# Order of low halves, evictions and copies, the second expert's rows and POOL's gates in a two-layer hybrid decoder trunk

## The reference, cut to what matters

```python
for l in range(2):
    h = rmsnorm(x, norm_mix[l])
    qa, ka, va, qb, kb, vb, qi, ki, wi, qc, kc, vc, g = split(h @ w_in[l])
    o_a = stick_breaking_attention(qa, ka, va)               # 4 heads
    o_b = dsa_attention(qb, kb, vb, qi, ki, wi, bias)        # top 64 keys per query, softmax
    o_c = sliding_window_attention(qc, kc, vc, sinks, bias)  # 8 heads, softmax with sinks
    gates = sigmoid(g + b_gate[l])
    merged = gates[0] * (o_a @ w_pa[l]) + gates[1] * (o_b @ w_pb[l]) + gates[2] * (o_c @ w_pc[l])
    x = x + merged @ w_out[l]
    x = x + cross_attention(rmsnorm(x), rmsnorm(mem), ...)   # 4 heads, 256 memory rows
    hf = rmsnorm(x, norm_ffn[l])
    x = x + (swiglu(hf) if l == 0 else moe_swiglu(hf))       # layer 1: top 2 of 8 experts
```

## Time and profile before

| what | us |
|---|---|
| median of 3 runs (1762.31 to 1764.25) | 1763.64 |
| the profiled execution, its own time | 1761.99 |
| its span, first to last instruction | 1760.4 |
| TensorE busy | 1702.5 (97%) |
| VectorE busy | 1391.7 (79%) |
| ScalarE busy | 1104.0 (63%) |
| POOL busy | 92.9 (5%) |

### The profile page before, as it was taken

The page is one execution under the profiler, slowest core; times in us unless marked ns, Lnnn a source line. Parts: engine busy times, 40 slices in busy tenths (PEclk is TensorE's granted clock), DMA queues, the critical chain, the costliest instruction groups (busy, mean ns, idle before and its releaser), DMA issues.

```text
span 1760.4 us, 22594 instructions
## 1 busy us (share of the span) xinstructions
PE 1702.5 (97%) x7816; PEld 1366.5 (78%) x7816; DVE 1391.7 (79%) x1367; ACT 1104.0 (63%) x1076; POOL 92.9 (5%) x73
## 2 busy tenths in 40 slices
PE   7999898999999999899999999999999999999999
PEld 5777777888777787777888888888888888888876
DVE  5799767545477987668898888888888888888897
ACT  4646355443355453557777777777777777777765
POOL 1100110000001001010000000000000000000440
PEclk9999999999999999999999999999999999999999
DMA  8533494554455335349999999999999999999985
GB/s 301 215 104 130 176 364 149 212 191 169 150 182 182 120 138 204 134 173 399 366 381 366 366 381 369 366 383 365 364 385 363 381 363 368 380 367 366 409 340 195
DMA packets 74113, 498.14 MB, mean 283 GB/s; under 512 B 8256, under 2 KB 9024, under 8 KB 17872
## 3 DMA queue, kind: packets, MB, share of 16 engines
q1 hardware_dynamic: 66560, 467.60, 69.4%
q0 software_dynamic: 7360, 29.87, 4.6%
q10 hardware_dynamic: 144, 0.03, 0.0%
HBM read 481.73 MB, written 15.73 MB: 283 GB/s over the span
## 4 chain that ended last, share of the span: by engine, by line
PE 83%; DVE 8%; ACT 3%; issue 2%; DVEq 2%; DMA 2%; POOL 0%; ACTq 0%; POOLq 0%; SPq 0%
PE ps L588 26%; PE ps L582 26%; PE ps L578 25%; DVE w_lo L416 3%; PE ps L804 1%; ACT w_hi L411 1%; DVE w_lo L1022 1%; PE ps L508 1%; PE ps L1348 1%; DMA rows_of_experts<-scratch,row_no 1%; DVE st L1673 0%; DMA z<-rows_of_experts 0%; DVEq L1676 0%; PE ps L1271 0%; DMA raw<-in_layer_tiles 0%
## 5 line engine op out<-in xcount | busy, mean ns | idle before, releaser
L1022 DVE TENSOR_TENSOR w_lo<-raw,w_hi 128x2048 fp32r<-128x2048 f32 x168 | 391.6, 2332 | 65.9 <-ACT w_hi L939 65.8
L578 PE MATMUL ps<-w_hi,hT_hi 128*128 128x512 f32 (+1 forms) x1520 | 427.1, 403 | 10.4 <-ACT hT_hi L550 4.6
L1022 DVE TENSOR_TENSOR w_lo<-z,w_hi 128x2048 fp32r<-128x2048 f32 x168 | 386.8, 2304 | 45.8 <-ACT w_hi L939 44.7
L588 PE MATMUL ps<-w_lo,hT_hi 128*128 128x512 f32 (+1 forms) x1520 | 413.2, 394 | 7.2 <-DVE w_lo L416 7.1
L582 PE MATMUL ps<-w_hi,hT_lo 128*128 128x512 f32 (+1 forms) x1520 | 413.0, 394 | 1.0 <-DVE hT_lo L557 0.9
L939 ACT ACTIVATE w_hi<-z 128x2048 fp32r<-128x2048 f32 x168 | 321.7, 1915 | 43.2 <-PE ps L588 38.3
L588 PEld LDWEIGHTS ps<-w_lo,hT_hi 128*128 128x128 f32 x1520 | 283.5, 189 | 77.3 <-DVE w_lo L416 9.9
L582 PEld LDWEIGHTS ps<-w_hi,hT_lo 128*128 128x128 f32 x1520 | 284.1, 189 | 70.2 <-DVE hT_lo L557 2.1
L939 ACT ACTIVATE w_hi<-raw 128x2048 fp32r<-128x2048 f32 x168 | 321.0, 1911 | 25.5 <-PE ps L588 25.5
L578 PEld LDWEIGHTS ps<-w_hi,hT_hi 128*128 128x128 f32 x1520 | 272.5, 189 | 67.8 <-ACT hT_hi L550 5.5
L416 DVE TENSOR_TENSOR w_lo<-raw,w_hi 128x2048 fp32r<-128x2048 f32 (+2 forms) x111 | 248.3, 2242 | 77.0 <-ACT w_hi L411 75.2
(11 more groups left out here) (295 smaller groups left out, 993.8 us busy)
## 6 DMA issues: line engine op xcount, KB each, us to landing
z<-in_moe_tiles SPq DMA_DIRECT2D x168, 1024.0 KB, 4.9
raw<-in_moe_tiles SPq DMA_DIRECT2D x168, 1024.0 KB, 4.9
raw<-in_layer_tiles SPq DMA_DIRECT2D x68, 1024.0 KB, 4.9
raw<-in_dense_tiles SPq DMA_DIRECT2D x33, 1024.0 KB, 4.8
rows_of_experts<-z POOLq DMA_DIRECT2D x1, 8704.0 KB, 40.6
raw<-in_layer_tiles SPq DMA_DIRECT2D x8, 512.0 KB, 3.4
z<-rows_of_experts POOLq DMA_DIRECT2D x8, 512.0 KB, 8.1
rows_of_experts<-z POOLq DMA_DIRECT2D x7, 512.0 KB, 6.8
```

The costliest lines, as they stand in the source:

```text
L578: pe.matmul(acc, hi[:, k, cols], wh, start=start and j == 0, stop=False)
L588: ins = pe.matmul(acc, hi[:, k, cols], wl, start=False, stop=stop and j == len(hk) - 1)
L1022: v.tensor_tensor(w_lo[:, ring, :], moe_raw(p), w_hi[:, ring, :].bitcast(F32), ALU.subtract) \
```

## The change

Ten edits. (1) POOL's gate product is a `tensor_tensor` with the gate's column broadcast to 1024 columns, no longer a `tensor_scalar`. (2) `dve_linear` can evict the first tile ahead of the low half; the first input block of layer 1 uses it. (3) For the first expert, TensorE turns the second expert's rows behind the fourth chunk, no longer behind the third, and (4) ScalarE and VectorE take them behind the fourth chunk, no longer inside it. (5) TensorE does an idle product in bank 0 ahead of the second tile's turning and one behind it, and one behind the logits in place of two. (6) At the start of layer 0 ScalarE and (7) VectorE take the first half of the turned input ahead of the first slot's split. (8) In the mixers one low half moves from behind the row maxima of the second tile to in front of them. (9) In the merge, pb's second block evicts its first tile without a low half in front, and the low halves of the pc slots come one eviction later each. (10) In cross-attention VectorE's copy moves ahead of a low half.

```diff
--- before.py
+++ after.py
@@ -345,7 +345,7 @@
                 pool.wait_ge(sem(f"y_back{k}"), 16)
                 if j:
                     pool.wait_ge(sem("x_part"), i + 1)
-                pool.tensor_scalar(yg[:, k, :], yg[:, k, :], g_other[:, j, i:i + 1], None, ALU.mult)
+                pool.tensor_tensor(yg[:, k, :], yg[:, k, :], bc(g_other[:, j, i:i + 1], [P, D]), ALU.mult)
                 pool.drain()
                 pool.tensor_tensor(x_sb[:, i, :], x_sb[:, i, :], yg[:, k, :], ALU.add).then_inc(sem("x_part"), 1)
 
@@ -618,12 +618,13 @@
                 pe_block_slot(pe, s + n, k0 + 4 * h, h == 0, h == per - 1 or plan[s + n][1] == KC, blk0[name, l] + b, x_lo,
                               hi, lo, between[1] if between and between[0] == n else None)
 
-        def dve_linear(v, cnt, name, l, take, limit, b0=0, b1=None):
+        def dve_linear(v, cnt, name, l, take, limit, b0=0, b1=None, take_first=False):
 
             s, nblk, per = slots_of(name, l)
             for b in range(b0, b1 or nblk):
                 last = s + (b + 1) * per - 1
-                ahead(dve_split_to, v, cnt, last - 1, limit)
+                if not take_first:
+                    ahead(dve_split_to, v, cnt, last - 1, limit)
                 blk = blk0[name, l] + b
                 v.wait_ge(sem("tile0_done"), blk + 1)
                 take(b, 0).then_inc(sem("evac"), 1)
@@ -859,8 +860,11 @@
                 pe_moe_chunk(pe, ip, par, 0, 0, ("hg_L", n + 1))
             pe_moe_chunk(pe, ip, par, 0, 1)
             pe_moe_chunk(pe, ip, par, 1, 0)
-            pe_turn_rows(pe, n + 1)
+            if not first_expert(ip, par):
+                pe_turn_rows(pe, n + 1)
             pe_moe_chunk(pe, ip, par, 1, 1)
+            if first_expert(ip, par):
+                pe_turn_rows(pe, n + 1)
             with pe.Fori(2, N_MOE // 2) as u:
                 pe_moe_chunk(pe, ip, par, u, 0)
                 pe_moe_chunk(pe, ip, par, u, 1)
@@ -928,7 +932,9 @@
                 chunk(0, 0)
             chunk(0, 1, None if first else "y")
             chunk(1, 0)
-            chunk(1, 1, "rows")
+            chunk(1, 1, None if first else "rows")
+            if first:
+                hook("rows")
             with fori(2, N_MOE // 2) as u:
                 chunk(u, 0)
                 chunk(u, 1)
@@ -1385,10 +1391,10 @@
                     if i == 1 and b == 0:
                         pe_turn_tile(pe, l, 0)
 
-        def pe_idle_products(pe, n):
+        def pe_idle_products(pe, n, bank=7):
 
             for _ in range(n):
-                pe.matmul(ps[:, 7, :], ident, x_sb[:, 0, 0:NB], start=True, stop=True)
+                pe.matmul(ps[:, bank, :], ident, x_sb[:, 0, 0:NB], start=True, stop=True)
 
         def pe_program(pe):
 
@@ -1445,9 +1451,11 @@
                     pe_turn_half(pe, "mix", x_sb, 0)
                 if l == 0:
                     pe_dense(pe, FFN0[0], N_DENSE, turn_next)
+            pe_idle_products(pe, 1, 0)
             pe_turn_tile(pe, L - 1, 1)
+            pe_idle_products(pe, 1, 0)
             pe_logits(pe, 1)
-            pe_idle_products(pe, 2)
+            pe_idle_products(pe, 1)
             pe.wait_ge(sem("chosen"), 1)
             pe.matmul(ps[:, 6, 0:8], before_tri, chosen[:, 0, :], start=True, stop=True)
             pe.matmul(ps[:, 6, 8:16], ones, chosen[:, 0, :], start=True, stop=False)
@@ -1598,8 +1606,8 @@
                     act.wait_ge(sem("ident_in"), 16)
                     act.activation(warm, ident[:, 0:1], ACT.Copy)
                     act.wait_ge(sem("gains"), 16)
+                    act_hi_gain(act, "mix", l, hT_hi, part=(0,))
                     act_split_to(act, cnt, s0 + 1)
-                    act_hi_gain(act, "mix", l, hT_hi, part=(0,))
                     act.wait_ge(sem("x1_in"), 16)
                     act_squares(act, x_sb, 0, "mix_squares")
                     act_hi_gain(act, "mix", l, hT_hi, part=(1,))
@@ -1766,6 +1774,7 @@
             dve_split_to(v, cnt, g0 + 3)
             dve_gate(v, l, 0, 0)
             dve_masked(v, l, 0, 1, between=0)
+            dve_split_to(v, cnt, g0 + 4)
             dve_row_max(v, l, 1)
             dve_split_to(v, cnt, g0 + 5)
             dve_topk_rounds(v, 0, 1)
@@ -1850,7 +1859,9 @@
                     last = s + (b + 1) * per - 1
                     blk = blk0[name, l] + b
                     for i in range(TT):
-                        if not (j == 1 and b == 0 and i == 1 or j == 2 and b == 1 and i == 1):
+                        if j == 1 and b == 1 and i == 1:
+                            dve_split_to(v, cnt, min(last + RING - 1, lim))
+                        elif not (j == 1 or j == 2 and b == 1 and i == 1) or b == i == 0:
                             dve_split_to(v, cnt, min(last + RING - 1 + i, lim))
                         if i == 0:
                             v.wait_ge(sem("tile0_done"), blk + 1)
@@ -1933,9 +1944,9 @@
             v.drain()
             dve_cross_probs(v, l, 0)
             dve_cross_max(v, l, 1)
-            dve_split_to(v, cnt, s + 3)
             v.wait_ge(sem("x_probs_T"), 2 * l + 1)
             v.tensor_copy(xPT[:, 1, :, 0:P], psXT[0][:, 1, :, :]).then_inc(sem("x_pT_dve"), 1)
+            dve_split_to(v, cnt, s + 3)
             dve_cross_probs(v, l, 1)
             v.wait_ge(sem("x_probs_T"), 2 * l + 2)
             v.tensor_copy(xPT[:, 1, :, P:S], psXT[1][:, 1, :, :]).then_inc(sem("x_pT_dve"), 1)
@@ -2063,10 +2074,9 @@
                 s0 = blocks["in", l]
                 if l == 0:
                     v.wait_ge(sem("gains"), 16)
+                dve_lo_gain(v, "mix", l, hT_hi, hT_lo, part=(0,))
                 if l == 0:
                     dve_split_to(v, cnt, s0 + 1)
-                dve_lo_gain(v, "mix", l, hT_hi, hT_lo, part=(0,))
-                if l == 0:
                     v.wait_ge(sem("mix_squares"), 2)
                     dve_rsqrt(v, "mix", D, norm_rs[:, 0:2])
                     dve_lo_gain(v, "mix", l, hT_hi, hT_lo, part=(1,))
@@ -2081,7 +2091,7 @@
                 v.drain()
                 if l == L - 1:
                     v.wait_ge(sem("rows_put"), 16)
-                dve_linear(v, cnt, "in", l, take_in(v), gate0[l], b1=1)
+                dve_linear(v, cnt, "in", l, take_in(v), gate0[l], b1=1, take_first=l > 0)
                 if l == 0:
                     v.wait_ge(sem("mem0_in"), 16)
                     v.wait_ge(sem("mem_squares"), 2)
```

## The result

The change makes the kernel slower: 1770.69 us median (1769.02 to 1771.03, 7 runs) against 1764.25 (1761.79 to 1767.38, 7 runs) for the kernel before on the same chip. The ratio is 1.0034, 95% interval 1.0024 to 1.0043, which is +6.0 us, between +4.2 and +7.6. The forecast was 1769.5, +5.9.

The account below looks back on a forecast made before the run. TensorE is busy 1702.5 of 1760.4 us, so order can win only its 58 us of standing and clock loss behind stops. Terms -0.8, -1.6, -0.3, +2.9, +5.7 sum to +5.9, so 1769.5 us; range 1762 to 1774.

Parts of the forecast that it names:

- Start: Start of layer 0: copying the turned input before the split lets TensorE start earlier; -0.8 us, bounds -1.3 and 0.
- First eviction of layer 1: First block of layer 1: TensorE's wait moves to the second eviction; 0, bounds -0.3 and +0.3 us.
- Mixers: Low half before the maxima: TensorE's gain is lost at the evictions behind them; 0 per layer, bounds -0.5 and +0.5 us.
- Merge: Merge, both layers: shorter waits for evictions and less half-speed time; together -1.6 us, bounds -4.6 and 0.
- Cross-attention: VectorE's copy runs earlier, but TensorE still needs ScalarE's copy; 0, bounds 0 and +0.6 us per layer.
- Router: Second tile's logits and ranks: VectorE's chain decides and a 0.34 us wait goes; -0.3 us, bounds -1.0 and +0.8.
- Rows: First expert: fetch wait of 1.38 us goes, TensorE stands 3.0 for ScalarE's queued split; +2.9 us, bounds +1.5 and +4.4.
- Gates: Last expert's tail: eight POOL operations hold VectorE 15.7 us, TensorE loses 9.5; +5.7 us, bounds +0.5 and +8.
- that sign: In the tail: the prediction is wrong if TensorE's waits stay near 4 us, where around 9 us was expected.
- rival C: Rows and tail: more half-speed stretches, and POOL between every pair of low halves; +1.5 and +2, 1773 us; chance 0.18.
- Rival A: POOL's gates: the broadcast product holds VectorE no longer than the scalar one; 5.2 us less, 1764.3; chance 0.2.
- Rival B: Mixers, merge, router: TensorE's clock decides and half of 17 us comes back, 1761.0 us; chance 0.12.

Follow-up runs that it names:

- experiment 7: The change without its gates, rows and idle-product edits, against the kernel before: 1762.14 us, ratio 0.9988.
- experiment 8: Experiment 7 with cross-attention left as before, against the kernel before: 1761.70 us, ratio 0.9989.
- experiment 11: Experiment 10 without the edits in the mixers and cross-attention, against the kernel before: 1759.76 us, ratio 0.9980.
- experiment 9: The kernel before with the change's idle products around the second tile's turning and four behind the logits: 1764.32 us, ratio 1.0000.
- experiment 6: The kernel before with only the change's idle-product edits in the router: 1764.91 us, ratio 1.0007.
- experiment 5: The kernel before with the second expert's rows turned behind the fourth chunk but taken inside the fifth, between splits: 1761.10 us, ratio 0.9984.
- experiment 1: The kernel before with only POOL's gate products made products of two tensors, one a broadcast column: 1767.42 us, ratio 1.0017.
- experiment 2: The kernel before with POOL's gate products made products of two whole tensors, gates left out of the output: 1768.98 us, ratio 1.0023.
- experiment 4: The kernel before with only the change's edits to the second expert's rows, turned and copied behind the fourth chunk: 1766.99 us, ratio 1.0019.
- experiment 12: Experiment 10 with the idle products of experiment 9, against the kernel before: 1759.65 us, ratio 0.9977.
- experiment 10: Experiments 5 and 7 together, with scalar gate products and the router as before, against the kernel before: 1760.64 us, ratio 0.9984.

## Why the prediction was right

By its own steps:

- **Start: right in mechanism, too small in size.** -1.06 in the profile, -1.2 and -0.7 in experiments 7 and 8, forecast -0.8; against the seven kernels with the old start it is nearer -1.7, beyond the bound of -1.3. TensorE's first products wait for the split, which follows the copy. They start 5.55 us behind the input in each of the six kernels with the edit, and 6.1 to 6.7 behind it (6.3 before) in the others; the rest is the clock, which comes up to 1.00 between 16.0 and 18.6 us, and between 16.6 and 19.7 in the others:

```profile
9.45 1.57 ACT L550 ACTIVATE hT_hi<-ps,gains 128x256 fp32r<-128x256 f32 x4 [6.14 <-PE ps L508]
10.89 1.93 ACT L411 ACTIVATE w_hi<-raw 128x2048 fp32r<-128x2048 f32 x1
...
12.96 2.05 PE L578 MATMUL ps<-w_hi,hT_hi 128*128 128x512 f32 x4 [3.61 <-ACT w_hi L411]
```

- **First eviction of layer 1: right.** The wait of the earlier trace rows moves to the second eviction and keeps its length, 1.45 for 1.49.

- **Mixers: right, and the trace shows it as forecast.** The 3.39 us behind the maxima are gone, and TensorE waits 3.42 us for the eviction behind them; the product of the probabilities starts at 143.42 where it started at 143.71, with TensorE 0.3 us earlier all along:

```profile
139.57 1.65 PE L578 MATMUL ps<-w_hi,hT_hi 128*128 128x512 f32 x4 [3.42 <-DVE z L1701]
...
143.42 3.36 DVE L1841 TENSOR_TENSOR scratch<-scratch,st 128x3072 f32<-128x3072 f32 x1
```

It said "two or three shorter waits instead of 3.4"; it is one of the same length. The 0 holds for the mixers themselves. But the three kernels that have the edit and the old router lose 0.9 to 1.0 us in the router (experiment 11), which the prediction did not look for.

- **Merge: right.** -0.55 and -0.82, forecast -0.7 and -0.9; none of the six kernels with the edit has a half-speed stretch in either merge, seven of the other eight have one in layer 0's and four in layer 1's. VectorE loses both ties with POOL (3.44 and 3.35 us for a low half), and the waits are 1.16, then 0.85, with 0.46 behind, where 0.95, 1.05 and 0.85 were worked out:

```profile
201.74 3.44 DVE L416 TENSOR_TENSOR w_lo<-raw,w_hi 128x2048 fp32r<-128x2048 f32 x1
...
205.23 1.21 PE L588 MATMUL ps<-w_lo,o_hi 128*128 128x512 f32 x4 [1.16 <-DVE w_lo L416]
...
210.09 1.17 PE L578 MATMUL ps<-w_hi,o_hi 128*128 128x512 f32 x4 [0.85 <-DVE scratch L1873]
```

- **Cross-attention: right**, 0 by experiment 8, as near as it can tell.

- **Router: wrong.** The step reads: "-0.3; bounds -1.0 and +0.8". It was +1.66, and +1.2 alone. That the clock may fall in the stop of 3 us was in it, and that VectorE's chain gains 0.34; but it followed VectorE alone. Behind the ranks TensorE has two idle products and the first expert's turning in its own order, and at half speed it is later than VectorE. Experiment 9 shows the cause by taking the stop away, experiment 6 that a later wait for the fetch can hide half of it (1.6 of 2.8), a cover that the rows' edit removes. Whether a part of the +1.66 comes with the mixers' edit, no run shows.

- **Rows: right**, in mechanism and size. Wait 2.91 (forecast 3.0), +3.1 in the profile and +3.4 alone (forecast +2.9). Experiment 5 shows that it is the split behind the copy.

- **Gates: the mechanism right for VectorE, wrong in part for TensorE, and the size not right.** "Now eight operations hold VectorE like an add: 1.3 for the first [...] and 7 x 2.05, 15.7 in all" is the term that was mis-sized. The excess was 12.2: the first product held VectorE for 0.6 (a low half of 2.89), the other products for 1.35, and the product with a broadcast column lasts 1.90 and not 2.40. TensorE lost 6.5 us against the 9.5 worked out and the 3.8 before, and not all of it by waiting. Its waits were 4.8 us, where the prediction looked for about 9 and called itself wrong if they stayed near 4: by that sign it was nearer to wrong than to right. The other 1.7 us are a half-speed stretch, a term that the sum for the gates left out and only rival C had.

Rival A put the product's price at 0.58; the 1.35 measured lies in the middle between that and the 2.05. The trace contradicts rival A as it stood. It also contradicts the Trainium skill, SBUF — State Buffer, "Who interferes with whom", by which the issue order and not the form of an instruction decides who blocks, so that a scalar product would lock the ports as an add does. Exchanging them cost +3.0 alone (+1.6 to +4.6) where the prediction had about +1 by that rule, and before, experiment 1 and experiment 2 show three prices for three kinds of product: 0.58, 1.35 and 1.84.

Rival B did not come: behind the start the clock is at 1.2 GHz for 34.1 us in all, against 30.7 before. Its list of the stretches left out two of 6.8 us in the cross-attentions. Of rival C, the stretch behind the rows' stop and one behind a stop in the tail are there, but the waits are shorter than it had them.

The sum of the parts measured alone (+3.0 +3.4 +1.2 -2.1 = +5.5) is near the +6.0 of the whole. That the forecast came within 1.2 us of the measured median is in part luck: 3.0 too much for the gates against 2.0 too little for the router, and within the gates a half-speed stretch of 1.7 that made up for part of the waits that did not come.

## What to carry to other kernels

When an engine's item is moved to the end of a stage, look at what its queue holds behind it: the copy of the rows costs 3 us with a split behind it and gains 2.8 one split later. Follow every engine's own queue behind a stop, TensorE's at half speed above all, and not only the chain that ended last before. And price a POOL instruction beside VectorE by the time it takes alone and by what it reads, not by the fact that it is elementwise.

## What the runs showed of the hardware

POOL and VectorE hold each other up in different ways for the two forms. An add or a product of two tensors alternates with the low halves: one goes, the other waits, 3.95 for a product of 1.90 and 4.25 for an add of 2.40. A scalar product lets VectorE pass and is itself drawn out, over two or three low halves; in the profile of experiment 8:

```profile
1669.22 7.01 POOL L348 TENSOR_SCALAR scratch<-scratch,headsT 128x1024 f32<-128x1024 f32 x1
1676.39 2.52 POOL L350 TENSOR_TENSOR x_sb<-x_sb,scratch 128x1024 f32<-128x1024 f32 x1 [0.16 <-issue]
1678.88 7.02 POOL L348 TENSOR_SCALAR scratch<-scratch,headsT 128x1024 f32<-128x1024 f32 x1
```

With 7.0 us the adds come 9.7 us apart, and TensorE waits 2.3 to 2.4 us there (experiments 4, 5, 8 and 12); with 4.9 us for two of the products, as in the profile of before, the first adds come 7.4 to 7.5 apart, and it waits 3.6 to 3.8, or 2.5 with a half-speed stretch of 3.4 us (experiments 6, 10 and 11). Which of the two a run gets differs among kernels that have the same instructions there, and is worth 1.0 to 1.5 us. The gap of 8.1 to 9.6 us behind POOL's first product is there with each kind of product (8.47 in experiment 2, 9.56 after the change); the prediction had it go with the scalar one. It lies inside POOL's drain between the product and the add (L349 before), which takes 12.3 to 12.6 us the first time in all thirteen kernels that have it, and 6.4 to 9.5 later. What the drain waits for stays open.

The half-speed stretches behind TensorE's stops move. The same edit-free place (cross-attention of layer 0) shows a wait of 2.6 or 3.2 us and a step of 0 to +1.0 in different executions, and an edit in the mixers of layer 1 goes with a lower clock one and two stages on. In the router, filling the stop with products took such a loss away (the clock is 1.00 in experiments 9 and 12).
